# The norm and turning of four row blocks inside the out-projection, and four of its weight tiles scaled by VectorE

## The reference

```python
merged = jax.nn.sigmoid(gr) * (y_ret @ ret_proj[l]) + jax.nn.sigmoid(gf) * (y_fox @ fox_proj[l])
x = x + g1[:, None, :] * (merged @ w_out[l])
h2 = modulate(rms_norm(x, norm2_w[l]), sh2, sc2)
ffn = (jax.nn.silu(h2 @ w_gate[l]) * (h2 @ w_up[l])) @ w_down[l]
x = x + g2[:, None, :] * ffn
```

## Time and profile before

| | us |
|---|---|
| median of 3 runs | 1936.36 (1935.87 to 1937.72) |
| the profiled execution, its own time | 1936.59 |
| its span, first to last instruction | 1934.8 |
| PE busy in it | 1853.2 |
| DVE, ACT, POOL busy | 1115.0, 681.7, 1004.2 |

### The profile page before, as it was taken

The page is one execution under the profiler, slowest core; times in us unless marked ns, Lnnn a source line. Parts: engine busy times, 40 slices in busy tenths (PEclk is TensorE's granted clock), DMA queues, the critical chain, the costliest instruction groups (busy, mean ns, idle before and its releaser), DMA issues.

```text
span 1934.8 us, 24236 instructions
## 1 busy us (share of the span) xinstructions
PE 1853.2 (96%) x8634; PEld 1536.4 (79%) x8634; DVE 1115.0 (58%) x1649; ACT 681.7 (35%) x1222; POOL 1004.2 (52%) x615
## 2 busy tenths in 40 slices
PE   4989999999999999999999997989999999999998
PEld 3778778888888778878888886877888888878887
DVE  6834764455554566766565547674455555555636
ACT  5633240323223333223332231174444434442123
POOL 1776642435261677775536346249888878800000
PEclk8999998999999999999999998999999999999999
DMA  8056631112021544434222124612444434399864
GB/s 328 33 174 193 231 100 35 45 28 61 23 55 25 188 151 158 168 104 161 70 76 70 43 79 181 238 68 67 146 158 153 163 134 159 122 379 364 302 222 172
DMA packets 186530, 272.18 MB, mean 141 GB/s; under 512 B 10281, under 2 KB 122825, under 8 KB 186193
## 3 DMA queue, kind: packets, MB, share of 16 engines
q1 hardware_dynamic: 176466, 243.20, 37.3%
q10 hardware_dynamic: 9984, 27.91, 4.0%
HBM read 194.23 MB, written 76.85 MB: 140 GB/s over the span
## 4 chain that ended last, share of the span: by engine, by line
PE 80%; DVE 5%; DMA 5%; POOL 4%; issue 3%; ACT 2%; SPq 0%; ACTq 0%; DVEq 0%; POOLq 0%
PE ps L1188 43%; PE ps L1655 10%; PE ps L1656 10%; PE ps L1657 10%; PE ps L1578 2%; PE ps L1267 1%; PE ps L1269 1%; PE ps L1268 1%; DMA b_da<-f_units 1%; POOL b_a_wu L979 1%; DMA b_mix<-ret_merge 1%; DMA ret_merge<-b_macc 1%; POOL b_a_raw L983 1%; DVE b_ada_acc L2523 1%; ACT b_act_q L2231 0%
## 5 line engine op out<-in xcount | busy, mean ns | idle before, releaser
L1188 PE MATMUL ps<-b_hT,b_w_split 128*128 128x512 f32 x2528 | 631.1, 398 | 3.7 <-POOL b_w_split L970 2.0
L1188 PEld LDWEIGHTS ps<-b_hT,b_w_split 128*128 128x128 f32 x2528 | 463.9, 190 | 93.7 <-DVE b_rm L2402 2.2
L1655 PE MATMUL ps<-b_act_q,b_wu 128*128 128x512 f32 x616 | 240.3, 390 | 9.0 <-DVE b_act_q L2402 4.6
L1657 PE MATMUL ps<-b_act_q,b_wu 128*128 128x512 f32 x616 | 239.8, 389 | 0.0
L1656 PE MATMUL ps<-b_act_q,b_wu 128*128 128x512 f32 x616 | 239.6, 389 | 0.0
L967 POOL TENSOR_TENSOR b_spare<-b_w_stage 1x1 f32<-1x1 f32 x66 | 21.7, 328 | 416.3 <-PE ps L1188 329.4
L1150 POOL TENSOR_TENSOR b_wu<-b_raw,b_wu 128x512 fp32r<-128x512 f32 x110 | 165.5, 1514 | 57.0 <-ACT b_wu L2207 56.8
L968 POOL TENSOR_SCALAR b_w_split<-b_w_stage 128x1024 fp32r<-128x1024 f32 x66 | 182.6, 2766 | 0.0
L2402 DVE TENSOR_TENSOR b_macc<-ps,b_macc 128x512 f32<-128x512 f32 x188 | 122.6, 687 | 79.9 <-PE ps L1269 49.6
L970 POOL TENSOR_TENSOR b_w_split<-b_w_stage,b_w_split 128x1024 fp32r<-128x1024 f32 x66 | 161.5, 2447 | 5.5
L1655 PEld LDWEIGHTS ps<-b_act_q,b_wu 128*128 128x128 f32 x616 | 115.6, 188 | 35.2 <-issue 10.1
(11 more groups left out here) (285 smaller groups left out, 3443.6 us busy)
## 6 DMA issues: line engine op xcount, KB each, us to landing
f_units<-b_fu SPq DMA_DIRECT2D x70, 512.0 KB, 2.6
b_w_stage<-in_w_in SPq DMA_DIRECT2D x53, 512.0 KB, 4.0
down_units_d<-b_wd SPq DMA_DIRECT2D x66, 256.0 KB, 2.0
b_da<-f_units SPq DMA_DIRECT2D x11, 1536.0 KB, 6.4
b_macc<-in_ada_w SPq DMA_DIRECT2D x32, 512.0 KB, 4.5
b_dr<-down_units_d SPq DMA_DIRECT2D x14, 1024.0 KB, 9.8
b_da<-f_units SPq DMA_DIRECT2D x7, 2048.0 KB, 8.0
b_wd<-in_w_down SPq DMA_DIRECT2D x11, 1024.0 KB, 5.0
```

The lines of the kernel that those rows point to most:

```text
L1188: return pe.matmul(o, l, r, start=start, stop=stop)
L1655: pe.matmul(o, l[0], r[0], start=begin and at == 0, stop=False, skip_group_check=go_on)
L1657: return pe.matmul(o, l[1], r[0], start=False, stop=at == end, skip_group_check=go_on)
```

## The change

Five edits, in the order of the program:

1. Near the start, SP issues the transfer of gate weight pair 3 right after pair 2, ahead of four stores.
2. In the merge stretch, VectorE scales weight tiles 4 to 7 of the out-projection and makes their lo parts (`SCALE_AT`, `LOW_AT`); GpSimd no longer does. ScalarE makes a merge's hi part before it issues the next `mix_load`, and the hi parts of tiles 4 to 6 stand one to two merges later. The second to fourth transfers of x wait for merges 5, 7 and 9 (counted from 0) where they waited for nothing.
3. In the out-projection, the turning of row blocks 0 to 3 stands after `t6 q1` (d 0 to 3) and after `t7 q0` (d 4 to 7). Rows 0 to 6 are squared ahead; row 7 is squared, rooted and scaled by itself later. Turning of row blocks 4 to 7 stands after unit 3 (d 0 to 3) and after unit 7 (d 4 to 7), and VectorE does `mod_block(1, d)` for d 4 to 7.
4. Units 0 to 3 live in `w_split`, `wo_ab` and `wo_de` in place of four `act_q` tiles.
5. For that reason the loads of `da` 0, 1, 2 wait for 2, 5, 6 used units where they waited for 1, 3, 5, and the hi parts of `db` for 2, 4, 4 in place of 2, 4, 6.

```diff
@@ SP
             for b in (0, 2, 1, 3):
                 if b == 2:
                     a_raw_load(2)
+                    a_raw_load(3)
                 for p in range(2):
                     park(p, b)
-                if b == 1:
-                    a_raw_load(3)
...
-            sp.wait_ge(m_sum, MERGE_AT[KT - 1, 1] + 1)
-            sp.dma_start(resid[:, 0:2, :], x_v[:, 0:2, :]).then_inc(s_xagain, 16)
+            def resid_load(i, merges):
+                sp.wait_ge(m_sum, merges)
+                sp.dma_start(resid[:, 2 * i:2 * i + 2, :], x_v[:, 2 * i:2 * i + 2, :]).then_inc(s_xagain, 16)
+            resid_load(0, MERGE_AT[KT - 1, 1] + 1)
             wo_load(7)
             for i in range(1, 4):
-                sp.dma_start(resid[:, 2 * i:2 * i + 2, :], x_v[:, 2 * i:2 * i + 2, :]).then_inc(s_xagain, 16)
+                resid_load(i, MERGE_AT[KT - 1, 1] + 2 * i)
@@ shared
+        HIGH_AT = {1: 4, 3: 5, 6: 6, 7: 7}
+        LOW_AT = {3: 4, 4: 5, 7: 6, 8: 7}
+        SCALE_AT = {0: 4, 2: 5, 5: 6, 6: 7}
...
-                eng.wait_ge(u_used, AFTER_QK + Q7 * (FT - 1) + 2 * g + 1)
+                eng.wait_ge(u_used, AFTER_QK + Q7 * (FT - 1) + (2, 5, 6)[g])
@@ GpSimd
             wo_high(3)
             wo_low(3)
-            wo_scale(4)
-            for i in range(5, KT):
-                wo_scale(i)
-                wo_low(i - 1)
-            wo_low(KT - 1)
@@ PE
             for t in range(6, 8):
                 for q in range(2):
...
+                    if (t, q) in ((6, 1), (7, 0)):
+                        for d in range(4):
+                            row_transposes(0, d if t == 6 else d + 4)
...
-            for d in range(KT):
-                row_transposes(0, d)
-            for d in range(4):
-                row_transposes(1, d)
+            pe.wait_ge(h_mdd, AFTER_QK + 5)
             for n in UNIT_RUN:
...
-                    if n == 0 and k == KT // 4:
-                        for d in range(4, KT):
-                            row_transposes(1, d)
                     last = gate_up_part(n, n, u, k)
                 last.then_inc(u_used, 1)
+                if n in (3, Q7):
+                    for d in range(4):
+                        row_transposes(1, d if n == 3 else d + 4)
@@ ScalarE
             for m in range(len(MERGES)):
-                act.wait_ge(m_sum, m + 1)
+                merged_hi(m)
                 if m in after:
                     mix_load(after[m])
-                merged_hi(m)
-                if m in (0, 2, 4, 7):
-                    wo_high({0: 4, 2: 5, 4: 6, 7: 7}[m])
+                if m in HIGH_AT:
+                    wo_high(HIGH_AT[m])
...
+            for t in range(TT - 1):
+                row_square(t)
+                if t > 0:
+                    row_root(t - 1)
+                if t >= 2 and t - 2 not in POOL_ROWS:
+                    row_scaled(t - 2)
+            row_root(6)
...
             unit_hi(0)
+            row_scaled(6)
+            unit_hi(3)
+            row_square(7)
+            row_root(7)
+            row_scaled(7)
             for d in range(4):
                 mod_block(d)
@@ VectorE
             for m in range(11):
                 merge(m)
+                if m in SCALE_AT:
+                    wo_scale(SCALE_AT[m])
+                if m in LOW_AT:
+                    wo_low(LOW_AT[m])
...
+            for d in range(4):
+                mod_block(0, d)
+            mean(1, 6)
+            inverse(1, 5)
+            add_out(14)
+            for d in range(4, KT):
+                mod_block(0, d)
+            inverse(1, 6)
+            unit_low(0)
+            add_out(15)
+            unit_low(3)
+            mean(1, 7)
+            inverse(1, 7)
+            block_sums(1)
+            for d in range(4, KT):
+                mod_block(1, d)
+            unit_low(1)
+            block_sums(4)
+            unit_low(5)
+            block_sums(2)
+            unit_low(4)
+            block_sums(6)
+            unit_low(2)
+            unit_low(6)
```

More of the change, by code:

```diff
@@ L1645, in _, with row_transposes @@
                             last.then_inc(o_pj, 1)
+            def row_transposes(th, d):
+                bank = turn_bank(th, d)
+                if th == 0:
+                    if d == 0:
+                        pe.wait_ge(n_xn, TT + 2)
+                        pe.wait_ge(n_xp, 2)
+                        pe.wait_ge(o_acc, 12)
+                    elif d >= 4:
+                        pe.wait_ge(h_mdd, AFTER_QK + d - 3)
+                else:
+                    if d == 0:
+                        pe.wait_ge(n_xn, TT + TT - len(POOL_ROWS))
+                        pe.wait_ge(n_xp, len(POOL_ROWS))
+                        pe.wait_ge(o_acc, 16)
+                        pe.wait_ge(h_mdd, AFTER_QK + KT)
+                    elif d > 4:
+                        pe.wait_ge(h_mda, AFTER_QK + d - 4)
+                for b in range(4):
+                    last = pe.transpose(ps[:, bank, blk(b)], macc[:, 4 * th + b, blk(d)], ident)
+                last.then_inc(h_tr, 1)
             for t in range(6, 8):
@@ L2882, in _ @@
                 norm_steps(1, t)
-            for t in range(4, TT):
+            for t in range(4, 7):
                 for q in range(2):
```

105 lines of the change are left out of this document (51 added, 54 removed).

## The result

The changed kernel takes **1942.35 us** (median of 8 runs, 1940.99 to 1946.3) where the kernel before, on the same chip, takes 1936.57: a ratio of 1.0029, with a 95% interval of 1.0019 to 1.0040. That is 5.8 us more by the medians and 5.6 (3.7 to 7.7) by the ratio. Timed again beside three experiments it was 1.0037 (1.0023 to 1.0050). The forecast was 1949.0, 12.4 us more: the direction is right, the size about double. The profiled execution took 1943.17 us, span 1941.1, 6.3 more than that of before.

What follows compares the result with a forecast made beforehand. PE, 80% of the chain of waits, was taken as the bound. 1936.6 + 10.0 (early turning 15.0 less merges 5.0) + 2.0 down-projection + 0.4 unit 3 = 1949.0 us; 8 in 10 range 1941 to 1957.

Steps and rivals of the forecast that it cites:

- Merges, -5.0: Merge stretch: scaling and lo parts moved to VectorE bring the last merge's sum 5.0 us earlier.
- three even cycles: Merge stretch: merges 5, 7 and 9 follow a cycle of 9.6 us, with 6.5 for the transfer.
- the final 1239.5: Last merge's sum: taken at 1239.5; the count gave 1241, or 1238 without the last wait for x.
- since one load of x runs beside every cycle: Merge stretch: reason for taking 6.5 us per mix transfer, between 4.5 alone and 7.4 beside the loads of x.
- Turning starts 29.9 us behind the last sum: GpSimd's gate-weight chain to scaled row 3 stays 29.9 us, so PE pauses some 13 us before turning.
- +15.0 from there: From the turning's start to the units' last lo part: early turning costs 15.0 us, ends 13 and 17.
- +0.4 for unit 3: Units behind the turning: PE waits 0.4 us for the late lo part of unit 3.
- the wait costs nothing: First turning: rows 0 to 3 scaled before PE asks, so PE passes warm; 1933.7 us, chance 0.03.
- Down-projection, +2.0: Loads of da: the second waits two more units, 5.4 us, and its later issue costs PE 2.0 us.
- My lower end of 0: Down-projection: another queue uses the time and gives it back, so the later loads cost 0.
- Early gate weights, 0: Gate weight pair 3 issued earlier: taken as 0, up to 1.5 us if it slows the pair ahead.
- The port rule: GpSimd's rounding of tile 3 would block two-input VectorE operations: new scaling 2.5 us later, sum 1951.5; forecast did not follow it.

Runs made afterwards that it cites:

- e8: Changed kernel with the loads of x issued at once behind merge 4, not one with each second merge: 1941.05 us, ratio 1.0029.
- e12: e9 with the loads of x issued at once behind merge 4: ratio 0.9965 to the kernel before.
- e1: Changed kernel with the turning of rows 0 to 3 put back behind the out-projection's last matmul on PE: 1938.78 us, ratio 1.0014.
- e6: Changed kernel, norm of rows 0 to 3 ahead of gate weights on every engine, ScalarE's later squares and unit 0's hi part woven between weights: 1931.59 us.
- e13: Kernel before, da loads put off to units 4, 7, 7 of the last pair and ScalarE's splits to 4, 6, 6: 1941.84 us, ratio 1.0031.
- e7: Kernel before with only SyncE's fourth gate-weight load moved ahead of the parked stores: ratio 0.9996.
- e3: Changed kernel with the merge part undone, early turning and the units' new homes kept: 1949.47 us, ratio 1.0072.
- e2: Kernel before with the merge part alone, including spread loads of x and ScalarE's hi-part order: 1931.42 us, ratio 0.9973.
- e11: Kernel before with only the earlier hi part and spread loads of x; GpSimd still scales and splits tiles 4 to 7: ratio 1.0009.
- e9: e6 with rows 4 to 7 turned behind units 0 and 3, row 7's statistics earlier, row 5 scaled before weight tile 1: 1928.02 us.

## Why the prediction came out at double

Point by point, by its own steps:

- **Merges, -5.0.** Measured -5.2 (S - A). Counted from A (1.75 added to the changed kernel's times), the count's marks hold within 1 us: merge 9 near 1215.4 for 1215, the adds from 1222.1 for 1221.5. The pattern inside is not the one forecast: VectorE waited once for 5.27 us, at merge 6, and 2.37 at merge 9, where three even cycles were counted. And the final 1239.5 is in part luck: the count itself gave 1241, and I took a value between that and 1238; it came out at 1239.3. The argument that the spread loads help, "since one load of x runs beside every cycle", has the sign wrong: loads at once are about 2 us better (e8, e12), because the spread puts the last load of x in front of VectorE's first add (3.64 us).
- **Turning starts 29.9 us behind the last sum.** Measured 29.9 (1237.5 to 1267.43), pause 12.07 for some 13.
- **+15.0 from there, +0.4 for unit 3.** Measured +14.9 at E, and the wait for unit 3 is 0.4. The last lo part ends 48.5 us behind the turning's start; 47.4 was foretold. The size holds, and so do the steps of the sum: the last block is turned at T + 28.6 for 28, and VectorE needs 19.9 from there for 19.4. The reason given for it holds only in part. I wrote that PE stands "with 48 matmuls still undone" as the cause; e1 shows that this is 4.2 of the 14.9, and the late place of rows 4 to 7 the rest. The time of the rival "the wait costs nothing" (1933.7, or 1931.7 without the 2.0 for the down-projection) came in e6 (1931.59), but there more than the wait was moved.
- **Down-projection, +2.0.** This is the step that failed. The sentence "a later issue costs only the bytes not moved meanwhile", priced at 1.35 to 2.7, took every microsecond of later issue as bytes lost to PE. But the second load was 22.2 us under way before and 16.1 after, and in e13 the second, issued later still, landed in 6.5: most of the 22.2 was queueing behind other bytes, which a later issue spares. PE's wait went from 3.32 to 2.52, and the term measured between 0 and -1, so the sum had 2 to 3 us too much here. My lower end of 0 came close.
- **Early gate weights, 0.** e7: nothing that can be told.
- **The rest of the gap.** Of the 6.8 us between the forecast 12.4 and the timed 5.6, the down-projection is 2 to 3 and the stretch 0.8 (9.6 for 10.4). The sum of the marks, +9.6 and up to -1, is 8.6 to 9.6 us, where the timed runs give 5.6 (3.7 to 7.7) and 7.2 (4.5 to 9.7). So about 2 to 3 us have no mechanism here. Part is the spread of the timing, with an A that wanders by microseconds: e3 has +15.3 - 1 by the marks and +13.9 by the runs, e2 -4.9 and -5.2. But with -1 for the new waits, the runs lie below the marks in all nine timings of kernels with the early turning, by 0.2 to 3.0 us, 1.3 on average, and at nearly nothing on average in the other six. What that is stays open.
- **The port rule.** GpSimd's rounding ran from 1170.20 to 1173.41. Inside it VectorE's scaling took 2.05 us, against 1.22 for that size alone, and the two-input lo part at 1172.68 took 0.68. By the Trainium skill (SBUF — State Buffer, the section on SBUF's two separate sides) both would have stood until 1173.41. The trace disagrees, as the rows before did; for GpSimd's two-input operations it agrees (2.85 us in e11, and 0.69 for the same operation, at 1236.85, once GpSimd is idle).

## What to carry to other kernels

Before work is moved ahead of a wait, ask which engine must deliver there and what its own list holds in front of it: here GpSimd's fourteen weight operations stood before two rows, and reordering them on all engines (e6, e9) turned a loss of 0.3% into a gain of 0.3 to 0.45%. When a pause is filled, look for the next in line: 48 matmuls put into a pause of 12 us gave back 4. The better lever was the last block turned, which E followed by 27.9 to 28.0 us in nine profiles. And measure a stretch from a mark at its own start, since the way up to it differed by 5.8 us between executions while the whole stretch repeated within 0.3; read the parts inside it from more than one profile.
